# Two row products moved from VectorE to GpSimd and ScalarE, and one weight load released earlier

## The reference, cut to what matters

```
h = h + mixed @ w_mix_out[l]
h = h + peer_ffn(rmsnorm_2(h, norm2_g[l]), ...)
# in peer_ffn, per token: 8 heads, each picks 16 experts
qh = (x_blk @ w_q)...                       # queries, 8 heads
scores = einsum('thpc,hpnc->thpn', qh, skf) # against the sub-keys
...top 16 of 16x16 sums -> e_idx, g = softmax
u = expert_u[e_idx]; v = expert_v[e_idx]
a = gelu(einsum('td,thkd->thk', x, u))
return einsum('thk,thkd->td', g * a, v)
```

## Time and profile before

| | us |
|---|---|
| median of 3 runs | 1704.89 (1704.56 to 1705.18) |
| the profiled execution's own time | 1704.29 |
| span of the profile | 1702.5 |
| busy in the span: PE / DVE / ACT / POOL | 1592.4 / 1178.5 / 855.0 / 365.4 |
| mean granted TensorE clock | 0.989 |

### The profile page before, as it was taken

One profiled execution on the slowest core, in us unless ns is written; L12 is line 12 of the kernel. 1 busy time (PEld: TensorE's weight loads), 2 busy tenths in 40 slices (PEclk: granted clock), 3 DMA queues, 4 the chain that ended last, 5 costly groups with the idle time before them and its releaser, 6 DMA issues.

```text
span 1702.5 us, 20955 instructions
## 1 busy us (share of the span) xinstructions
PE 1592.4 (94%) x7940; PEld 1163.5 (68%) x7940; DVE 1178.5 (69%) x2066; ACT 855.0 (50%) x1564; POOL 365.4 (21%) x381
## 2 busy tenths in 40 slices
PE   9999999999999999999999999999987887888786
PEld 7888998888888899888889998655532232333232
DVE  6868766666686876666675557988777667767755
ACT  5556535434465663534455545655444445444443
POOL 0200000000120000000060001555574444444430
PEclk9999999999999999999999999999999999999999
DMA  7543554544544355454544457999999999999997
GB/s 282 202 150 128 194 199 166 193 179 182 197 175 160 125 180 210 165 192 182 196 180 157 168 196 273 417 427 427 426 427 427 427 427 427 427 427 427 427 427 316
DMA packets 67943, 464.47 MB, mean 273 GB/s; under 512 B 7929, under 2 KB 10113, under 8 KB 12930
## 3 DMA queue, kind: packets, MB, share of 16 engines
q0 software_dynamic: 37152, 268.45, 37.4%
q1 hardware_dynamic: 30400, 194.34, 31.0%
q10 hardware_dynamic: 290, 0.33, 0.1%
HBM read 462.04 MB, written 1.06 MB: 272 GB/s over the span
## 4 chain that ended last, share of the span: by engine, by line
PE 62%; DMA 23%; DVE 8%; ACT 3%; issue 2%; POOL 1%; SPq 1%; POOLq 0%; ACTq 0%; DVEq 0%
PE acc L673 12%; PE acc L675 11%; PE acc L674 11%; DMA row_w_lo<-in_peer_uv,arena 7%; DMA arena<-in_peer_uv,arena 6%; PE att L698 5%; PE acc L698 4%; PE acc L1847 4%; PE acc L1850 3%; DMA row_xa<-in_peer_uv,arena 3%; PE att L699 3%; DMA row_w_hi<-in_peer_uv,arena 2%; DMA row_w_lo<-in_peer_uv,small 2%; PE acc L699 2%; DVE w_lo L635 1%
## 5 line engine op out<-in xcount | busy, mean ns | idle before, releaser
L635 DVE TENSOR_TENSOR w_lo<-arena,w_hi 128x2048 fp32r<-128x2048 f32 x160 | 365.3, 2293 | 145.0 <-ACT w_hi L619 144.6
L619 ACT CAST w_hi<-arena 128x2048 fp32r<-128x2048 f32 x164 | 312.3, 1907 | 117.3 <-PE acc L675 96.6
L1992 ACT ACTIVATE arena<-arena,small 128x1 f32<-128x1 f32 x256 | 75.2, 294 | 252.2 <-DVE arena L2372 118.7
L2372 DVE SCALAR_TENSOR_TENSOR arena<-arena 128x1024 f32<-128x1024 f32 x107 | 130.7, 1224 | 76.0 <-DMA arena<-in_peer_uv,arena 76.0
L1847 PE MATMUL acc<-arena,diagonals 128*128 128x512 f32 x214 | 121.3, 650 | 47.1 <-ACT diagonals L2002 46.8
L673 PE MATMUL acc<-xa,w_hi 128*128 128x256 f32 x544 | 155.4, 286 | 0.0
L674 PE MATMUL acc<-xa,w_lo 128*128 128x256 f32 x544 | 153.8, 283 | 0.0
L675 PE MATMUL acc<-xa,w_hi 128*128 128x256 f32 x544 | 153.8, 283 | 0.0
L2614 POOL DMA_INDIRECT arena<-in_peer_uv,arena x107 | 117.2, 1096 | 137.2 <-PE acc L1850 130.3
L698 PE MATMUL acc<-xa,w_hi 128*128 128x512 f32 x384 | 138.2, 402 | 1.5 <-DVE arena L1412 1.5
L698 PE MATMUL att<-xa,w_hi 128*128 128x512 f32 x384 | 136.0, 398 | 0.0
(11 more groups left out here) (382 smaller groups left out, 3596.4 us busy)
## 6 DMA issues: line engine op xcount, KB each, us to landing
arena<-in_units SPq DMA_DIRECT2D x173, 1024.0 KB, 4.8
arena<-in_units SPq DMA_DIRECT2D x4, 512.0 KB, 7.6
arena<-in_bias SPq DMA_DIRECT2D x1, 2048.0 KB, 10.6
arena<-in_peer_uv,arena POOLq DMA_INDIRECT x107, 41.1
x_res<-in_x SPq DMA_DIRECT2D x2, 512.0 KB, 5.1
arena<-m_parked SPq DMA_DIRECT2D x2, 512.0 KB, 3.5
arena<-in_norm_mlp_g SPq DMA_DIRECT2D x2, 512.0 KB, 6.4
arena<-in_norm_g SPq DMA_DIRECT2D x2, 512.0 KB, 5.1
```

What stands on the lines that cost most here:

```text
L619: nc.scalar.copy(flat(w_hi, s), raw[HOME[g]]).then_inc(S["hi_ready"], 1)
L635: nc.vector.tensor_tensor(flat(w_lo, s), raw[HOME[g]], flat(w_hi, s).bitcast(F32), ALU.subtract).then_inc(S["lo_ready"], 1)
L2372: nc.vector.scalar_tensor_tensor(row, row, 1.0, hn[:, n // SLOTS, :], ALU.mult, ALU.mult, accum_out=dots[:, n:n + 1]).then_inc(S["rows_use ...
```

## The change

Three edits. First, PE's product of `mix` 1 with the second tile is put in another order: the third pass of all four `k` comes first, and a new signal behind it (`tile_done` of "remainders") releases SP's load of `pq` 4, which before waited for the whole product. Second, DVE takes the remainder of head 2's query weights (`split_lo` of `pq` 2) after the dot of row 4 and not after that of row 3. Third, DVE doesn't make the dots of rows 10 and 11 any more. POOL multiplies these two rows with the tokens (two tensor_tensor of 128x1024), after the gather of row 15 and ahead of the two small instructions of the norm, and ACT sums each product with a Copy that accumulates, at the head of `diagonal(10)` and `diagonal(11)`.

```diff
+PRODUCTS_BY_POOL = (10, 11)
...
             elif HOME[g] == RAW_RING + 3:
-                sp.wait_ge(S["unit_done"], at("unit_done", ("u", at_unit2["mix", 1])))
+                sp.wait_ge(S["tile_done"], at("tile_done", ("mix", "remainders")))
...
+            def remainders_of_mix(t, i, ks):
+                b, s, xh, xl = operands(at_unit2["mix", i], False)
+                lw = wlo(s, "T")
+                for k in ks:
+                    m = nc.tensor.matmul(b[t][:], xh[:, 4 * (i % 2) + k, t * P:(t + 1) * P], lw[:, k, :], start=i % 2 == 0 and k == 0, stop=False)
+                return m
+            def rounded_of_mix(t, i, ks):
+                b, s, xh, xl = operands(at_unit2["mix", i], False)
+                h, tok = whi(s, "T"), slice(t * P, (t + 1) * P)
+                for k in ks:
+                    nc.tensor.matmul(b[t][:], xh[:, 4 * (i % 2) + k, tok], h[:, k, :], start=False, stop=False)
+                    m = nc.tensor.matmul(b[t][:], xl[:, 4 * (i % 2) + k, tok], h[:, k, :], start=False, stop=i % 2 == 1 and k == 3)
+                return m
...
                 queries_of(0, range(8))
-                tile_of_mix(1, 1, range(1, 2))
+                remainders_of_mix(1, 1, range(3, 4)).then_inc(S["tile_done"], mark("tile_done", ("mix", "remainders")))
+                rounded_of_mix(1, 1, range(1))
                 turn_queries(0)
-                tile_of_mix(1, 1, range(2, 3))
+                rounded_of_mix(1, 1, range(1, 2))
...
-                tile_of_mix(1, 1, range(3, 4)).then_inc(S["unit_done"], mark("unit_done", ("u", at_unit2["mix", 1])))
+                rounded_of_mix(1, 1, range(2, 4)).then_inc(S["unit_done"], mark("unit_done", ("u", at_unit2["mix", 1])))
...
-                    tile_of_mix(1, 1, range(1))
+                    remainders_of_mix(1, 1, range(3))
...
             def diagonal(n):
                 d = dots[:, n:n + 1]
-                act.wait_ge(S["rows_used"], n + 1)
+                if n in PRODUCTS_BY_POOL:
+                    row = rows_ring[PLACE[n]][:, 0:D]
+                    act.wait_ge(S["iota"], at("iota", ("product", n)))
+                    nc.scalar.activation(row, row, ACT.Copy, accum_out=d).then_inc(S["ssq_ready"], mark("ssq_ready", ("dot", n)))
+                    act.wait_ge(S["ssq_ready"], at("ssq_ready", ("dot", n)))
+                else:
+                    act.wait_ge(S["rows_used"], n + 1 - sum(m <= n for m in PRODUCTS_BY_POOL))
...
             for n in range(ITEMS):
-                row_dot(n)
+                if n not in PRODUCTS_BY_POOL:
+                    row_dot(n)
...
-                elif n == 3:
+                elif n == 4:
                     split_lo(dve, at_unit2["pq", 2])
...
                 elif n == P_TOP - 1:
+                    for m in PRODUCTS_BY_POOL:
+                        row = rows_ring[PLACE[m]][:, 0:D]
+                        pool.wait_ge(S[f"gathered{PLACE[m]}"], 16 * (USES_BEFORE[m] + 1))
+                        nc.gpsimd.tensor_tensor(row, row, hn[:, 0, :], ALU.mult).then_inc(S["iota"], mark("iota", ("product", m)))
                     norm_pool(pool, "n2", 1)
```

## The result

The changed kernel takes 1708.94 us (median of 14 runs, 1707.87 to 1710.36) against 1704.03 of the kernel before beside it (14 runs, 1703.04 to 1706.04): a ratio of 1.0028, 95% interval [1.0021, 1.0036]. By the ratio that is 4.8 us slower, and just past the 0.2% that the prediction called no change. Its 1706.7 was 2.2 us too low; its range of 1704.0 to 1709.1 holds the time, by 0.2 us. The profiled execution has a span of 1706.1 us and a time of 1707.87, the lowest of the 14.

A forecast was written before the change was run, and what follows sets the result against it. From row 0's gather on, the kernel was taken as one DMA stream at 427 GB/s, so only its start or a stall could move the end. -0.4 + 2.2 = +1.8 gave 1706.7 us on the median, range 1704.0 to 1709.1.

The forecast's parts named there:

- The load released earlier: SP's last load, signalled 2.5 us sooner, moves before row 0's gather and no longer partly beside it: -0.4 us.
- The remainder: Head 2's remainder after row 4's dot: that dot fills DVE's 1.10 us wait for ACT, worth 0.
- The two products: POOL's products end late beside DVE's work; row 16's gather goes out at 1097.6, not 1094.80, and the stream stalls: +2.2 us.
- my walk: Step-by-step timing of POOL's two products beside DVE's two-input work, at 6.02 ns per element: done at 1091.9 and 1096.5.
- The sums on ACT: ACT, DVE and PE some 2 us late from row 12; row 20's gather still ready in time, so 0 cost.
- within 0.2%: Measured time within 0.2% (3.4 us) of the kernel before, counted as no change: chance 0.84.
- The second rival: POOL beside DVE needs 12 ns per element; row 16's gather at 1099.5, +3.35 to +4.1 us, 1708.2 to 1709.0; chance 0.17.
- The third: Late ACT sums or product 11 free rows 12 and 13's places too late, stalling rows 20 and 21: about 1706; chance 0.06.
- still starts with the number: Sign against the forecast: row 16's gather released by DVE's cast of head 1's number, not by POOL's own work.
- the second gap: Sign against the forecast: another gap in the DMA stream at rows 20 to 25.
- The standstill of some 2 us: Sign for the forecast: DMA engines stand still for some 2 us near 1098.
- B: Theory of the experiments: ACT's two sums and table load make ACT and PE late, delaying gathers of rows 18 to 21.

The follow-up runs named there:

- e1: Changed kernel without the third edit: no products on POOL, all dots on VectorE; ratio 0.9999 to the kernel before.
- e7: Changed kernel with one more wait on GpSimd, so its products start after VectorE's small 128x16 subtraction; ratio 1.0027 to the kernel before.
- e5: Changed kernel without ACT's sums: GpSimd multiplies rows 10 and 11, VectorE then makes their dots from the products; ratio 1.0023 to the kernel before.
- e4: Changed kernel without products on POOL: VectorE makes all dots, ACT still sums rows 10 and 11 on top; ratio 1.0022 to the kernel before.
- e6: Sums-only kernel (no POOL products) plus a one-element gelu that brings the table load into ACT's wait for row 10; ratio 1.0012 to the kernel before.
- e12: Sums-only kernel (no POOL products) plus 18 small matmuls on PE ahead of its wait for row 10's diagonal; ratio 1.0019 to the kernel before.
- e2: Changed kernel with head 1's small subtraction as a tensor_tensor with two memory inputs, not a tensor_scalar; ratio 1.0033 to the kernel before.
- e8: First two edits, with the third applied to twenty rows later in the stream and not to rows 10 and 11; ratio 0.9999 to the kernel before.
- e11: Kernel before with the third edit alone: two products on GpSimd, their sums on ScalarE; ratio 1.0031 to the kernel before.
- e9: Changed kernel with three rows (10, 11, 12) on GpSimd and ScalarE in place of two; ratio 1.0041 to the kernel before.

## Why the prediction was right and wrong, by its own steps

- *What bounds the kernel* was right: only the stretch around row 16 mattered. DVE's freed dots were worth nothing; DVE idled 4.95 us instead.
- *The load released earlier, -0.4*: 0. SP issued it at 1049.97, which is 1051.2 with the shift of 1.26 us, as forecast, and 1.05 MB of q1 had moved by 1055.9, before row 0's first packet. But row 0 alone then moved at 313 GB/s (1.02 MB from 1055.9 to 1059.15), where before it and the load's rest had moved at 383 together. The 0.65 that I took from above for the load's rest is mostly row 0's own slow start. e1's ratio is 0.9999.
- *The remainder, 0*: right (e1).
- *The two products, +2.2*: mis-sized and, more than that, mis-told; this is the step that failed. I had read L2565's 1169 and 2312 ns as sharing, both engines going on at lower rates, POOL at 6.02 ns per element and "DVE a tenth slower". In its place e7's rows show that one of the two runs for the whole of its instruction and the other stands. POOL, first to ask, ran at full speed; DVE's 16-column subtraction, which my walk gave no cost, stood 3.6 us. By itself this measured 3.9 us (e5), in place of 2.2. The Trainium skill (SBUF — State Buffer, section "SBUF: two separate sides") states it: the port pair shared by GpSimd and VectorE is "an exclusive lock, not a bandwidth split", held for a whole instruction. The 3.81, 3.39 and 2.33 us of the traces agree: each reaches to the end of the other engine's instruction and has at most its own time behind that.
- *The sums on ACT, "Hidden: 0, with 0.3 us to spare in the one case and over 2 in the other"*: wrong, the second step that failed. They cost 3.7 us where the number is in time (e4) and, within the noise, about 1 behind the stall (4.8 against e5's 3.9). I looked at row 20's gather alone. The places of rows 18 and 19 are released by PE's rows 10 and 11, just those whose diagonals the sums delay. The diagonal's delay was also added up wrongly: 1096.79 + 1.2 = 1098.0 holds the sum and not the table load of 1.28 us, though the text says that it now comes behind the sum. With it the diagonal ends at 1099.3, and that is e4's +43.99. PE came to row 10 2.4 us late and not 0.9. Moving the load away, which also kept the clock up, was worth 1.7 us (e6), and the lower clock cost 1.4 us of PE's time (e12).
- *The sum and the chances*: +1.8 forecast, 4.8 measured. The case "within 0.2%" with 0.84 was too sure. That the range holds 1708.94 is luck: its upper part was there for a rival that did not happen. The second rival gave the right time (1708.2 to 1709.0) with the wrong mechanism: not POOL was slow but DVE. The third, ACT and PE taking over, had 0.06 and half of the truth; what I held against it, that a stall at row 16 gives the margin back, fits the 3.9 and 3.7 us that together make only 4.8.
- *The signs named beforehand*: "both products take under 2.6 us" came true, by the profile row 16's gather "still starts with the number", and the thin stream at rows 17 to 21 is the second gap, some rows earlier than I had put it. All three were signs that the forecast was wrong. The standstill of some 2 us came as well (2.2 us), but out of DVE's late number and not out of POOL's own work, so it is no support for the walk.

What stays open: how much of B's 3.7 us is the clock. e12 gives PE's 1.4 us but no time; e6 moved the table load and the clock at once. Why the clock fell in the changed kernel and not in e2 and e5, with the same wait of PE, is open as well. No run beat the kernel before: without edit 3 the stretch loses 0.3 to 0.8 us, which is all that was to be had there.

## What to carry to other kernels

Before work goes from VectorE to an idle GpSimd, find out which VectorE instruction it will stand beside and what waits for that one. Count the product's whole duration as a delay to it, however small it is, unless, as in e8, the queue that it feeds has many entries ahead. And when a chain gets a new step on ScalarE, look at the first consumer behind it (here the places of rows 18 and 19), and place a table load where the engine waits anyway.

## What the runs showed of the hardware

- A VectorE instruction of 0.22 us took 1.62, 3.81 and 6.10 us beside one, two and three GpSimd products of 2.4 us. The max and index searches (MAX8 0.43, FIND_INDEX8 0.42, over 256 columns) that ran beside the same product were not held. Single-input arithmetic (TENSOR_SCALAR, f32 and uint32), two-input arithmetic and the dots were.
- GpSimd's first 128x1 instruction of the norm took 1.26 us just behind the products, beside VectorE's dot of row 8; in the kernel before it took 0.20. The hold works in both directions.

```profile
1087.99 0.20 POOL L785 TENSOR_TENSOR small<-small 128x1 f32<-128x1 f32 x1
```

- Behind waits of PE of 2.77 us (changed kernel, 1095 to 1097.3), 2.19 us (e4), 2.50 us (e7), 2.49 us (e11) and 5.05 us (e9) the granted clock was 0.50 for 2 us or more; behind waits of 2.78 us (e2), 2.76 us (e5) and 0.91 and 0.69 us (e6) it stayed at 1.00. A wait of the same length did and did not bring a fall.
